# Decoder block on 8 cores: tables of the second half built early and kept in DRAM, halo projections in another order

## The chip, the cores and the metric

The program runs on the 8 cores of one Trainium2 chip, the same program on each with other data and no traffic between cores. Each core computes 2048 tokens of one sequence (4 sequences, two cores for each). The metric is the device time in microseconds (us) of the slowest core.

## The reference

One decoder layer over tokens of width 1024. What is computed:

```
h = x + 0.5*SwiGLU_1(rmsnorm(x))            # width 2816
u = rmsnorm(h);  z = u @ W_in               # [conv GLU | q | k | v | merge gates]
A = conv module (GLU, causal depthwise conv 31 wide, LayerNorm, swish, C->D)
q, k = rotary(q, cos, sin), rotary(k, cos, sin)     # cos, sin of positions*inv_freq
B = 12 heads of 128, 3 groups with dilation 1, 4, 16;
    query t attends to t - j*dilation, j = 0..128;  groups merged by softmax denominators
h = h + W_o(sigmoid(gA)*yA + sigmoid(gB)*yB)
h = h + 0.5*SwiGLU_2(rmsnorm(h))
h = h + sigmoid(rmsnorm(h) @ W_pg) * (p @ W_pp);  y = rmsnorm(h)
```

The tokens just ahead of a core's own 2048 (128, 512 or 2048 of them by group) are needed as keys and values too. They are called the halo here. A core computes them itself from `xh`, the 2048 tokens before its own.

## The kernel before

All activations lie transposed, channels on 128 partitions and tokens along the free axis; `H` is the float32 residual, `U` its normed bf16 copy, each 8 tiles of 128 channels by 2048 tokens, worked on in blocks of 512 tokens. The kernel goes through stages in this order:

- **Halo part.** Load `xh`, FFN 1, RMSNorm into `U` (line 480). Then two rotary tables for the halo's tokens are built: `build_tables` (line 387) loads 1 MB of positions with an SP DMA, does twenty-one 128x2048 passes on DVE, of which the last is a multiply by a sign, and two Sin activations on ACT, into `cos2` and `sinS` (`t_71`, `t_72`; the positions are `t_74`). Lines 494 to 519 then run over 12 heads, and for each do a K projection with rotary (`proj_rot`, line 403: for each block of up to 512 tokens 8 matmuls, an ACT copy, a permuting matmul, three DVE operations), a store of the result to `khd` in DRAM, a V projection (`proj_v`, line 421: for each 128 tokens 8 matmuls of 128 columns and a copy out of PSUM that alternates between DVE and ACT), and a store to `vhd`. Heads 0 to 3 have a halo of 128 tokens, 4 to 7 of 512, 8 to 11 of 2048. Lines 521 to 533 compute the conv branch's 32 halo columns. A barrier follows.
- **Own part.** Load `xo`, FFN 1, RMSNorm, a barrier (546), `build_tables` for the core's own tokens (557), another barrier (558). Then the projections of head 0 (`proj_rot_g`, `proj_v_g`), and the attention of a head woven with the projections of the next. After this the conv, the merge, FFN 2, the last gates and the output.

Order is written out by hand: `Sched` (line 33) keeps one list per engine in program order, and each engine works its list in that order. An operation waits by semaphores for the earlier writers and readers of its tiles. A DMA is issued by its engine's list too, so one that waits holds up those behind it: plain loads and all stores are on SP's list, and weight loads, which cast float32 to bf16, are on POOL's (`pool_load`). A barrier makes the next operation of each engine wait for the last of all engines and for all DMAs so far. Weights come in chunks of 128 output columns (`load_w_chunk`, line 464) into a ring of 4 tiles in the halo part and of 3 in the own part: a chunk's load waits until the matmuls of the chunk in its tile are done. PSUM has 8 banks of one tile each, taken in turn.

Of the kernel before, what the change touches and what calls it, by code (L numbers as in the profile page):

```python
# [8 lines left out]
F32 = mybir.dt.float32  # L9
BF16 = mybir.dt.bfloat16  # L10
I32 = mybir.dt.int32
# [4 lines left out]
NT = 2048  # L16
# [8 lines left out]
GROUPS = ((1, 16), (4, 4), (16, 1))  # L25
# [166 lines left out]
def _build_body(nc, dbg):  # L192
    S = None
# [18 lines left out]
    yT = nc.dram_tensor("yT", [D, NT], F32, kind="ExternalOutput").ap()  # L212
    khd = nc.dram_tensor("khd", [12, 128, NT], BF16, kind="Internal").ap()
    vhd = nc.dram_tensor("vhd", [12, 128, 16, 128], BF16, kind="Internal").ap()
    dbg_out = None
    if dbg:
        dbg_out = nc.dram_tensor("dbg", [D, NT], F32, kind="ExternalOutput").ap()

    S = Sched(nc)
    A = Arena(nc, 229376)  # L220
# [3 lines left out]
    def set_pool(banks):  # L224
        ps_pool["banks"] = list(banks)
        ps_pool["i"] = 0

    def ps_next():
        bk = ps_pool["banks"]
        i = bk[ps_pool["i"] % len(bk)]  # L230
        ps_pool["i"] += 1
        return PS[i], ("ps", i)
# [17 lines left out]
    def sp_load(dst, src, key, grp):  # L250
        S.op("sp", lambda e: e.dma_start(out=dst, in_=src), writes=[key], dma=grp)

    def pool_load(dst, src, key, grp):
        S.op("pool", lambda e: e.dma_start(out=dst, in_=src), writes=[key], dma=grp)  # L254
# [20 lines left out]
    def checkpoint(name):  # L275
        if STOP == name:
            yv_ = yT.rearrange("(c p) t -> p c t", p=128)
            for c in range(8):
                S.op("sp", lambda e, c=c: e.dma_start(out=yv_[:, c, :], in_=H[:, c, :]),
                     reads=[("H", c, b) for b in range(NB)], dma="yout")  # L280
            S.finish()
            S.emit()
            raise _Stop()

    def mm(out, lhsT, rhs, start, stop, reads, writes):
        S.op("pe", lambda e: e.matmul(out, lhsT=lhsT, rhs=rhs, start=start, stop=stop), reads, writes)  # L286

    def act(out, in_, func, reads, writes, bias=None, scale=None):
        kw = {}
        if bias is not None:  # L290
            kw["bias"] = bias
        if scale is not None:
            kw["scale"] = scale
        S.op("act", lambda e: e.activation(out=out, in_=in_, func=func, **kw), reads, writes)  # L294

    def tt(eng, out, in0, in1, op, reads, writes):
        S.op(eng, lambda e: e.tensor_tensor(out=out, in0=in0, in1=in1, op=op), reads, writes)  # L297

    def stt(eng, out, in0, scalar, in1, op0, op1, reads, writes):
        S.op(eng, lambda e: e.scalar_tensor_tensor(out=out, in0=in0, scalar=scalar, in1=in1, op0=op0, op1=op1), reads, writes)  # L300

    def ts(eng, out, in0, s1, s2, op0, op1, reads, writes):
        if s2 is None:
            S.op(eng, lambda e: e.tensor_scalar(out=out, in0=in0, scalar1=s1, scalar2=None, op0=op0), reads, writes)  # L304
        else:
            S.op(eng, lambda e: e.tensor_scalar(out=out, in0=in0, scalar1=s1, scalar2=s2, op0=op0, op1=op1), reads, writes)  # L306

    def cp(eng, out, in_, reads, writes):
        if eng == "act":
            S.op(eng, lambda e: e.copy(out=out, in_=in_), reads, writes)  # L310
        else:
            S.op(eng, lambda e: e.tensor_copy(out=out, in_=in_), reads, writes)  # L312
# [74 lines left out]
    def build_tables(cos2, sinS, pcol0, tmp_f, tmp_i, tmp_k):  # L387
        sp_load(tmp_i[:], pos[:, pcol0:pcol0 + NT], "tmp_i", "tab")
        for tab, key, shift in ((sinS, "sinS", 0.0), (cos2, "cos2", math.pi / 2)):
            cp("dve", tab[:], tmp_i[:], ["tmp_i"], [key])  # L390
            ts("dve", tab[:], tab[:], invf, shift, ALU.mult, ALU.add, [key, "sm"], [key])
            ts("dve", tmp_f[:], tab[:], 1.0 / TWO_PI, None, ALU.mult, None, [key], ["tmp_f"])
            cp("dve", tmp_k[:], tmp_f[:], ["tmp_f"], ["tmp_k"])
            cp("dve", tmp_f[:], tmp_k[:], ["tmp_k"], ["tmp_f"])
            stt("dve", tab[:], tmp_f[:], -TWO_PI, tab[:], ALU.mult, ALU.add, ["tmp_f", key], [key])
            ts("dve", tmp_f[:], tab[:], math.pi, -TWO_PI, ALU.is_gt, ALU.mult, [key], ["tmp_f"])
            tt("dve", tab[:], tab[:], tmp_f[:], ALU.add, [key, "tmp_f"], [key])
            ts("dve", tmp_f[:], tab[:], -math.pi, TWO_PI, ALU.is_lt, ALU.mult, [key], ["tmp_f"])
            tt("dve", tab[:], tab[:], tmp_f[:], ALU.add, [key, "tmp_f"], [key])
            act(tab[:], tab[:], AF.Sin, [key], [key])  # L400
        ts("dve", sinS[:], sinS[:], sgn, None, ALU.mult, None, ["sinS", "sm"], ["sinS"])
# [16 lines left out]
            tt("dve", t2[:, 0:n], pw[:, 0:n], sinS[:, tsl], ALU.mult, [pwk, "sinS"], [t2k])  # L418
            tt("dve", dst[:, o0:o0 + n], t1[:, 0:n], t2[:, 0:n], ALU.add, [t1k, t2k], [(dst_key, o0 // BL)])

    def proj_v(wt, wk, dst, dst_key, tile_starts, d, vring_keys=None):
        for i, st0 in enumerate(tile_starts):
            pv, pvk = ps_next()
            bs = sorted({(st0 + d * q) // BL for q in (0, 127)})
            bs = list(range(bs[0], bs[-1] + 1))
            for c in range(8):
                mm(pv[:, 0:128], U[:, c, st0:st0 + 127 * d + 1:d], wt[:, c, :],
                   c == 0, c == 7, [wk] + [("U", c, b) for b in bs], [pvk])
            cp("act" if i % 2 else "dve", dst[:, i, :], pv[:, 0:128], [pvk], [(dst_key, i)])

    def proj_rot_g(wt, wk, dst, dst_key, t0, ntok, cos2, sinS, qb_ring, t_ring):
        for o0 in range(0, ntok, BL):
# [31 lines left out]
    def load_w_chunk(ring, col0, ncol=128):  # L464
        wt, wk = ring.next()
        wt = wt[:, 0:8 * ncol].rearrange("p (c n) -> p c n", c=8)
        pool_load(wt, w_in_v[:, :, col0:col0 + ncol], wk, "%s%d" % wk)
        return wt, wk

    QOFF, KOFF, VOFF, GOFF = 2048, 2048 + 1536, 2048 + 3072, 2048 + 4608  # L470
# [11 lines left out]
    cos2 = A.alloc([128, NT], F32)  # L482
    sinS = A.alloc([128, NT], F32)
    tmp_f = A.alloc([128, NT], F32)
    tmp_i = A.alloc([128, NT], I32)
    tmp_k = A.alloc([128, NT], I32)
    build_tables(cos2, sinS, 0, tmp_f, tmp_i, tmp_k)
    checkpoint("p0b")
    wring = Ring(A, "w", int(os.environ.get("KW", "4")), [128, 8 * 128], BF16)
    qb_ring = Ring(A, "qb", 2, [128, BL], BF16)  # L490
    t_ring = Ring(A, "t", 4, [128, BL], F32)
    kst_ring = Ring(A, "kst", 2, [128, NT], BF16)
    vst_ring = Ring(A, "vst", 2, [128, 16, 128], BF16)
    for g, (d, nbl) in enumerate(GROUPS):
        nh = 128 * d
        for j in range(4):
            head = 4 * g + j
            if head < int(os.environ.get("KSKIP", "0")):
                continue
            wt, wk = load_w_chunk(wring, KOFF + head * 128)  # L500
            kst, kstk = kst_ring.next()
            proj_rot(wt, wk, kst, kstk, NT - nh, nh, cos2, sinS, qb_ring, t_ring)
            if not os.environ.get("KNOSTORE"):
              S.op("sp", lambda e, kst=kst, head=head, nh=nh: e.dma_start(out=khd[head, :, 0:nh], in_=kst[:, 0:nh]),
                 reads=[(kstk, i) for i in range((nh + BL - 1) // BL)], writes=[("khd", head)], dma="hstk%d" % kstk[1])
            if head == 0:
                checkpoint("p0c")
            wt, wk = load_w_chunk(wring, VOFF + head * 128)
            vst, vstk = vst_ring.next()
            starts = [NT - nh + r for r in range(d)]  # L510
            proj_v(wt, wk, vst, vstk, starts, d)
            if not os.environ.get("KNOSTORE"):
              S.op("sp", lambda e, vst=vst, head=head, d=d: e.dma_start(out=vhd[head, :, 0:d, :], in_=vst[:, 0:d, :]),
                 reads=[(vstk, i) for i in range(d)], writes=[("vhd", head)], dma="hstv%d" % vstk[1])
            if head == 0:
                checkpoint("p0d")
            if head == 11:
                checkpoint("p0e")
            checkpoint("p0h%d" % head)
    sg_ring = Ring(A, "sg", 2, [128, BL], F32)  # L520
    for c in range(8):
        wa, wak = load_w_chunk(wring, c * 128)
# [27 lines left out]

    cos2 = A.alloc([128, NT], F32)
    sinS = A.alloc([128, NT], F32)
    mark3 = A.off
    tmp_f = A.alloc([128, NT], F32)
    tmp_i = A.alloc([128, NT], I32)
    tmp_k = A.alloc([128, NT], I32)
    build_tables(cos2, sinS, NT, tmp_f, tmp_i, tmp_k)
    S.barrier()
    A.off = mark3
    set_pool([0, 1, 2, 3])  # L560
    wring = Ring(A, "w", 3, [128, 8 * 128], BF16)
    qb_ring = Ring(A, "qb", 2, [128, BL], BF16)
# [125 lines left out]
    wring = Ring(A, "w", 3, [128, 8 * 128], BF16)  # L688
# [64 lines left out]
    wring = Ring(A, "w", 2, [128, 8 * 128], BF16)  # L753
# [70 lines left out]
    for b in range(NB):  # L824
# [21 lines left out]
        for c in range(8):  # L846
# [3 lines left out]
                 reads=[("H", c, b)], dma="yout")  # L850
# [89 lines left out]
```

How the kernel before makes its waits and increments, by code:

```python
                def body(eng):  # L122
                    waited = {}
                    for o in self.ops[e]:
                        ws = {}
                        for d in o.deps:
                            if not self._needs(o, d):
                                continue
                            if d.is_dma:
                                key, sem, val = "d_" + d.grp, self.groups[d.grp][0], d.val
                            else:
                                key, sem, val = "s_" + d.eng, sems[d.eng], d.count
                            if waited.get(key, 0) >= val:
                                continue
                            if key not in ws or ws[key][1] < val:
                                ws[key] = (sem, val)
                        for key, (sem, val) in ws.items():
                            eng.wait_ge(sem, val)
                            waited[key] = val
                        inst = o.fn(eng)
                        if o.is_dma:
                            inst.then_inc(self.groups[o.grp][0], 16)
                        elif o.need_inc:
                            inst.then_inc(sems[e], 1)
```

## Time and profile before

| | us |
|---|---|
| median of 2 runs | 3450.42 (3449.57 to 3451.27) |
| profiled execution | 3456.62 |
| its span on the slowest core (core 4) | 3455.1 |
| spans of the 8 cores | 3432.3 to 3455.1 |

| engine | busy us | share of the span |
|---|---|---|
| PE matmul | 2759.9 | 80% |
| DVE | 1382.4 | 40% |
| ACT | 818.9 | 24% |
| POOL | 190.4 | 6% |

The shares are averages over stages that have different limits. What counts below are the stretches in which PE stands still, and what ends them. Times inside the execution are given in us from the start of core 4's span.

### The profile page before, as it was taken

To read this page: it belongs to the slowest core of one execution; us is meant where nothing else is said; L and a number is where in the kernel's file an instruction comes from. 1 tells how busy PE (TensorE), PEld (TensorE's weight loads), DVE (VectorE), ACT (ScalarE), POOL (GpSimd) and SP (SyncE) were. 2 spreads that over 40 slices of the span, in tenths; PEclk is the share of its full clock that TensorE was granted. 3 is DMA by queue.
4 is the path that set the end of the run, shared out by engine and by line. 5 is a ranking of instruction groups with operands and counts; after the bars stand their busy time and mean duration, and the time that the engine had idled before them with its cause. 6 is when DMAs were issued, how large, how long until landed. Compare 5 with 4: busy or idle time off the path is not lost.

```text
span 3455.1 us, 41479 instructions; the slowest of 8 cores (3432.3 to 3455.1 us)
## 1 busy us (share of the span) xinstructions
PE 2759.9 (80%) x14139; PEld 1305.8 (38%) x14360; DVE 1382.4 (40%) x2050; ACT 818.9 (24%) x1744; POOL 190.4 (6%) x228
## 2 busy tenths in 40 slices
PE   4999993655999991787777677747749989999977
PEld 1444440441444440454454433313324434444422
DVE  4131338424232337567667710130043353313267
ACT  3101012113101003222222244344421121010144
POOL 0000000120000000000000000000001010000010
PEclk9999995876999995999898888979979989999988
DMA  8131202877122100221121021112124252222042
GB/s 175 25 49 25 31 1 28 87 99 156 26 48 37 19 1 13 31 32 20 29 32 20 16 28 17 15 12 19 10 24 41 28 72 45 37 38 31 1 43 98
DMA packets 222233, 134.67 MB, mean 39 GB/s; under 512 B 165584, under 2 KB 204880, under 8 KB 219728
## 3 DMA queue, kind: packets, MB, share of 16 engines
q0 software_dynamic: 207488, 93.57, 23.6%
q1 hardware_dynamic: 14544, 38.44, 3.4%
q8 instruction: 124, 2.03, 0.2%
q14 instruction: 77, 0.63, 0.1%
HBM read 211.65 MB, written 13.89 MB: 65 GB/s over the span
## 4 chain that ended last, share of the span: by engine, by line
PE 69%; DVE 12%; ACT 9%; DMA 5%; issue 4%; SPq 0%; ACTq 0%; DVEq 0%; POOL 0%; POOLq 0%
PE ps L286 69%; ACT t L294 8%; DVE t L300 4%; DVE t L297 3%; DVE t L329 2%; DMA t<-w_in 2%; DVE t L660 2%; DMA t<-xh 1%; DMA t<-xo 1%; DVE t L312 1%; DMA t<-vhd 1%; DVE t L306 0%; ACT t L310 0%; DMA t<-w_co 0%; SPq L317 0%
## 5 line engine op out<-in xcount | busy, mean ns | idle before, releaser
L286 PE MATMUL ps<-t,t 128*128 128x512 bf16 (+1 forms) x14139 | 2759.9, 352 | 679.6 <-ACT t L294 319.4
L286 PEld LDWEIGHTS ps<-t,t 128*128 128x128 bf16 x14360 | 1305.8, 105 | 2133.1 <-issue 986.9
L297 DVE TENSOR_TENSOR t<-t,ps 128x512 bf16<-128x512 f32 (+3 forms) x688 | 388.4, 569 | 1175.6 <-PE ps L286 897.3
L294 ACT ACTIVATE t<-ps 128x512 f32<-128x512 f32 (+2 forms) x712 | 379.3, 534 | 1761.2 <-PE ps L286 1690.6
L300 DVE SCALAR_TENSOR_TENSOR t<-ps,t 128x512 f32<-128x512 f32 x292 | 202.0, 692 | 257.7 <-PE ps L286 254.9
L294 ACT ACTIVATE t<-t 128x512 bf16<-128x512 f32 (+1 forms) x260 | 159.7, 644 | 394.4 <-DVE t L300 130.9
L297 DVE TENSOR_TENSOR t<-ps,t 128x512 f32<-128x512 f32 (+1 forms) x240 | 154.1, 675 | 155.2 <-ACT t L294 153.7
L254 POOL DMA_DIRECT2D t<-w_in x124 | 108.9, 880 | 1784.0 <-PE ps L286 1264.7
L297 DVE TENSOR_TENSOR t<-t,t 128x512 bf16<-128x512 f32 (+5 forms) x228 | 191.2, 844 | 22.4 <-DVE t L297 0.7
L294 ACT ACTIVATE t<-t,t 128x128 bf16<-128x128 bf16 (+1 forms) x516 | 169.1, 415 | 26.3 <-DVE t L297 14.7
L300 DVE SCALAR_TENSOR_TENSOR t<-t,t,t 128x512 bf16<-128x512 f32 (+1 forms) x224 | 150.9, 746 | 3.0
L329 DVE RECIPROCAL t<-t 128x512 f32<-128x512 f32 x24 | 80.3, 3348 | 123.3 <-ACT t L294 123.3
L304 DVE TENSOR_SCALAR t<-ps,t 128x512 f32<-128x512 f32 x32 | 24.0, 752 | 232.1 <-PE ps L286 224.9
L310 ACT CAST t<-t 128x32 bf16<-128x32 f32 (+1 forms) x64 | 26.5, 414 | 188.8 <-DVE t L304 145.4
L294 ACT ACT_TABLE_LOAD x28 | 35.9, 1283 | 124.4 <-DVE t L297 79.3
L310 ACT CAST t<-ps 128x128 bf16<-128x128 f32 x136 | 36.2, 266 | 111.4 <-PE ps L286 111.4
L312 DVE CAST t<-ps 128x128 bf16<-128x128 f32 x140 | 38.6, 287 | 40.9 <-PE ps L286 40.8
L660 DVE RECIPROCAL t<-t 128x2048 f32<-128x2048 f32 x4 | 51.8, 12953 | 0.4
L312 DVE COPY t<-ps 128x128 f32<-128x128 f32 x128 | 36.4, 290 | 19.1 <-PE ps L286 10.5
L254 POOL DMA_DIRECT2D t<-w1g x12 | 10.6, 886 | 552.4 <-PE ps L286 541.1
L294 ACT ACTIVATE t<-ps,t 128x512 f32<-128x512 f32 x28 | 19.2, 687 | 16.1 <-PE ps L286 16.0
L845 DVE RECIPROCAL t<-t 128x512 f32<-128x512 f32 x4 | 13.4, 3353 | 21.7 <-ACT t L294 21.7
(26 smaller groups left out, 137.9 us busy)
## 6 DMA issues: line engine op xcount, KB each, us to landing
t<-w_in POOLq DMA_DIRECT2D x124, 256.0 KB, 5.5
t<-w1g POOLq DMA_DIRECT2D x10, 1024.0 KB, 10.9
t<-w1u POOLq DMA_DIRECT2D x10, 1024.0 KB, 16.2
t<-w1d POOLq DMA_DIRECT2D x10, 1024.0 KB, 14.4
t<-xh SPq DMA_DIRECT2D x8, 1024.0 KB, 19.5
t<-xo SPq DMA_DIRECT2D x8, 1024.0 KB, 20.4
yT<-t SPq DMA_DIRECT2D x32, 256.0 KB, 3.2
t<-w2g POOLq DMA_DIRECT2D x5, 1024.0 KB, 11.8
```

What stands on the lines that cost most here:

```text
L254: S.op("pool", lambda e: e.dma_start(out=dst, in_=src), writes=[key], dma=grp)
L286: S.op("pe", lambda e: e.matmul(out, lhsT=lhsT, rhs=rhs, start=start, stop=stop), reads, writes)
L294: S.op("act", lambda e: e.activation(out=out, in_=in_, func=func, **kw), reads, writes)
L297: S.op(eng, lambda e: e.tensor_tensor(out=out, in0=in0, in1=in1, op=op), reads, writes)
L300: S.op(eng, lambda e: e.scalar_tensor_tensor(out=out, in0=in0, scalar=scalar, in1=in1, op0=op0, op1=op1), reads, writes)
L304: S.op(eng, lambda e: e.tensor_scalar(out=out, in0=in0, scalar1=s1, scalar2=None, op0=op0), reads, writes)
L310: S.op(eng, lambda e: e.copy(out=out, in_=in_), reads, writes)
L312: S.op(eng, lambda e: e.tensor_copy(out=out, in_=in_), reads, writes)
L329: S.op("dve", lambda e, rt=rt: e.reciprocal(out=rt[:], in_=rt[:]), [rtk], [rtk])
L660: S.op("dve", lambda e: e.reciprocal(out=DEN[:], in_=DEN[:]), ["DEN"], ["DEN"])
L845: S.op("dve", lambda e, rt=rt: e.reciprocal(out=rt[:], in_=rt[:]), [rtk], [rtk])
```

## The change

- A DRAM tensor `tabd` for two 1 MB tables is added.
- In the halo part the loop over heads is split into two: first all 12 V projections with their stores, then all 12 K projections with theirs. The V tiles are all copied out of PSUM by ACT (`act_only`).
- Between the two loops `build_tables` is run for the own tokens, the tables are stored to `tabd`, and then it is run for the halo's tokens in the same tiles.
- In the own part `build_tables` and the barrier behind it are gone, and two loads from `tabd` stand in their place.

```diff
+    tabd = nc.dram_tensor("tabd", [2, 128, NT], F32, kind="Internal").ap()
...
-            cp("act" if i % 2 else "dve", dst[:, i, :], pv[:, 0:128], [pvk], [(dst_key, i)])
+            cp("act" if (i % 2 or act_only) else "dve", dst[:, i, :], pv[:, 0:128], [pvk], [(dst_key, i)])
...
-    build_tables(cos2, sinS, 0, tmp_f, tmp_i, tmp_k)
-    checkpoint("p0b")
-    wring = Ring(A, "w", int(os.environ.get("KW", "4")), [128, 8 * 128], BF16)
+    wring = Ring(A, "w", 4, [128, 8 * 128], BF16)
...
+            wt, wk = load_w_chunk(wring, VOFF + head * 128)
+            vst, vstk = vst_ring.next()
+            starts = [NT - nh + r for r in range(d)]
+            proj_v(wt, wk, vst, vstk, starts, d, act_only=True)
+            S.op("sp", lambda e, vst=vst, head=head, d=d: e.dma_start(out=vhd[head, :, 0:d, :], in_=vst[:, 0:d, :]),
+                 reads=[(vstk, i) for i in range(d)], writes=[("vhd", head)], dma="hstv%d" % vstk[1])
+    build_tables(cos2, sinS, NT, tmp_f, tmp_i, tmp_k)
+    S.op("sp", lambda e, t_=cos2: e.dma_start(out=tabd[0], in_=t_[:]), reads=["cos2"], writes=["tabd0"], dma="tst0")
+    S.op("sp", lambda e, t_=sinS: e.dma_start(out=tabd[1], in_=t_[:]), reads=["sinS"], writes=["tabd1"], dma="tst1")
+    build_tables(cos2, sinS, 0, tmp_f, tmp_i, tmp_k)
+    for g, (d, nbl) in enumerate(GROUPS):
+        nh = 128 * d
+        for j in range(4):
+            head = 4 * g + j
             wt, wk = load_w_chunk(wring, KOFF + head * 128)
             kst, kstk = kst_ring.next()
             proj_rot(wt, wk, kst, kstk, NT - nh, nh, cos2, sinS, qb_ring, t_ring)
...
-            wt, wk = load_w_chunk(wring, VOFF + head * 128)
-            vst, vstk = vst_ring.next()
-            starts = [NT - nh + r for r in range(d)]
-            proj_v(wt, wk, vst, vstk, starts, d)
...
-    mark3 = A.off
-    tmp_f = A.alloc([128, NT], F32)
-    tmp_i = A.alloc([128, NT], I32)
-    tmp_k = A.alloc([128, NT], I32)
-    build_tables(cos2, sinS, NT, tmp_f, tmp_i, tmp_k)
-    S.barrier()
-    A.off = mark3
+    sp_load(cos2[:], tabd[0], "cos2", "tld0")
+    sp_load(sinS[:], tabd[1], "sinS", "tld1")
```

SP's list in the halo part, before. `t_74` is the tile of positions, `t_86` and `t_87` are the staging tiles of K, `t_88` and `t_89` those of V.

```order
L317 DMA t_52<-xh 128x2048 x8
L251 DMA t_74<-pos 128x2048
L504 DMA khd<-t_86 128x128
L513 DMA vhd<-t_88 128x128
L504 DMA khd<-t_87 128x128
```

The same list from the last V stores on, with the change (`t_71` is `cos2`, `t_72` is `sinS`).

```order
L501 DMA vhd<-t_88 128x2048
L501 DMA vhd<-t_89 128x2048
L501 DMA vhd<-t_88 128x2048
L501 DMA vhd<-t_89 128x2048
L252 DMA t_74<-pos 128x2048
L504 DMA tabd<-t_71 128x2048
L505 DMA tabd<-t_72 128x2048
L252 DMA t_74<-pos 128x2048
L514 DMA khd<-t_86 128x128
```

The load of positions stood ahead of all stores of the part. It now stands behind the twelve V stores, and the second one behind the two table stores.

ACT's list with the change, from the copies of the last V heads on. The four rows on 128x2048 are the Sin activations of the two builds, and those that write `t_80` and `t_81` are the copies of the K projections.

```order
L311 CAST t_88<-ps 128x128 x16
L311 CAST t_89<-ps 128x128 x16
L295 ACTIVATE t_72<-t_72 128x2048
L295 ACTIVATE t_71<-t_71 128x2048
L295 ACTIVATE t_72<-t_72 128x2048
L295 ACTIVATE t_71<-t_71 128x2048
L295 ACTIVATE t_80<-ps 128x128
```

All V copies moved ahead of the Sin activations, and both builds' Sin activations stand ahead of the first K copy.

## Rows read from the trace of the kernel before

**Rows 1.** Chain that ended last (page, part 4): shares by engine

```profile
PE 69%; DVE 12%; ACT 9%; DMA 5%; issue 4%; SPq 0%; ACTq 0%; DVEq 0%; POOL 0%; POOLq 0%
```

**Rows 2.** Timeline, halo build: start us, us, engine, line, operation, count, [idle before <-releaser]

```profile
527.53 0.33 SPq L251 DMA_DIRECT2D t<-pos  x1
529.07 3.56 POOL L254 DMA_DIRECT2D t<-w_in  x4 [126.30 <-ACT t L294]
...
567.23 0.27 PE L286 MATMUL ps<-t,t 128*128 128x128 bf16 x1 [10.60 <-DVE t L300]
...
571.53 1.22 DVE L312 CAST t<-t 128x2048 f32<-128x2048 int32 x1
571.76 0.26 PE L286 MATMUL ps<-t,t 128*128 128x128 bf16 x1 [0.40 <-DVE t L300]
572.57 0.88 POOL L254 DMA_DIRECT2D t<-w_in  x1 [39.94 <-PE ps L286]
...
604.83 1.91 ACT L294 ACTIVATE t<-t 128x2048 f32<-128x2048 f32 x1 [13.20 <-DVE t L297]
...
607.05 1.99 PE L286 MATMUL ps<-t,t 128*128 128x128 bf16 x17 [35.03 <-ACT t L294]
```

**Rows 3.** Timeline, build of the own part

```profile
1332.65 5.39 DVE L300 SCALAR_TENSOR_TENSOR t<-t,t,t 128x512 bf16<-128x512 f32 x8
1338.77 0.33 SPq L251 DMA_DIRECT2D t<-pos  x1
1343.84 1.23 DVE L312 CAST t<-t 128x2048 f32<-128x2048 int32 x1 [5.79 <-DMA t<-pos]
...
1377.07 1.91 ACT L294 ACTIVATE t<-t 128x2048 f32<-128x2048 f32 x1 [13.42 <-DVE t L297]
...
1380.37 2.67 POOL L254 DMA_DIRECT2D t<-w_in  x3 [210.34 <-issue]
1385.05 3.57 PE L286 MATMUL ps<-t,t 128*128 128x512 bf16 x8 [61.84 <-DMA t<-w_in]
...
1389.56 3.93 PE L286 MATMUL ps<-t,t 128*128 128x512 bf16 x9 [0.95 <-ACT t L294]
```

**Rows 4.** Timeline, weight chunks of the conv halo, four issued together

```profile
735.38 3.50 POOL L254 DMA_DIRECT2D t<-w_in  x4 [8.72 <-PE ps L286]
743.21 1.01 PE L286 MATMUL ps<-t,t 128*128 128x128 bf16 x8 [7.42 <-DMA t<-w_in]
...
749.07 1.01 PE L286 MATMUL ps<-t,t 128*128 128x128 bf16 x8 [1.37 <-DMA t<-w_in]
```

**Rows 5.** Chain in order of time, last V projection: start us, us, what

```profile
726.08 8.39 PE ps L286 x129
```

**Rows 6.** Timeline, PE: ninth matmul of a 128-token K, blocks of 512 tokens

```profile
612.12 0.27 PE L286 MATMUL ps<-t,t 128*128 128x128 bf16 x1 [0.57 <-ACT t L294]
...
697.30 2.10 PE L286 MATMUL ps<-t,t 128*128 128x512 bf16 x9 [0.89 <-ACT t L294]
700.24 2.10 PE L286 MATMUL ps<-t,t 128*128 128x512 bf16 x9 [0.84 <-ACT t L294]
```

**Rows 7.** Stretches: engines' busy us (count), granted clock, DMA share, GB/s

```profile
572.00:606.00 34.00, 0.02 (x1) 0.00 (x0) 31.68 (x21) 4.36 (x3) 0.88 (x1) 0.50 0.08 8
620.00:640.00 20.00, 15.19 (x106) 9.42 (x109) 6.18 (x13) 2.86 (x7) 5.26 (x6) 0.70 1.04 99
657.00:667.00 10.00, 6.98 (x35) 3.17 (x36) 6.75 (x11) 1.79 (x3) 0.88 (x1) 1.00 0.01 1
607.05:734.70 127.65, 95.78 (x882) 65.95 (x889) 54.95 (x116) 23.31 (x63) 19.27 (x22) 0.88 0.69 86
1342.00:1343.00 1.00, 0.00 (x0) 0.00 (x0) 0.00 (x0) 0.00 (x0) 0.00 (x0) 0.50 0.95 401
```

**Rows 8.** Stores of the last four heads, 512 KB each, landing: vhd, then khd

```profile
DMA to landing us min/median/max: 2.7/2.7/3.5
DMA to landing us min/median/max: 4.0/4.3/4.9
```

**Rows 9.** Tile xh, eight loads of 1 MB: landing

```profile
DMA to landing us min/median/max: 5.3/19.5/32.5
```

**Rows 10.** Groups by form, 607 to 735 us

```profile
L310 ACT CAST t<-ps 128x128 bf16<-128x128 f32 x40 | 10.6, 266 | 41.8 <-PE ps L286 41.8
```

More of the change, by code:

```diff
@@ L419, in proj_rot, with proj_v @@
             tt("dve", dst[:, o0:o0 + n], t1[:, 0:n], t2[:, 0:n], ALU.add, [t1k, t2k], [(dst_key, o0 // BL)])
-    def proj_v(wt, wk, dst, dst_key, tile_starts, d, vring_keys=None):
+    def proj_v(wt, wk, dst, dst_key, tile_starts, d, vring_keys=None, act_only=False):
         for i, st0 in enumerate(tile_starts):
@@ L497, in _build_body @@
             head = 4 * g + j
-            if head < int(os.environ.get("KSKIP", "0")):
-                continue
+            wt, wk = load_w_chunk(wring, VOFF + head * 128)
[12 more added lines that the diff above has]
+            head = 4 * g + j
             wt, wk = load_w_chunk(wring, KOFF + head * 128)
@@ L502, in _build_body @@
             proj_rot(wt, wk, kst, kstk, NT - nh, nh, cos2, sinS, qb_ring, t_ring)
-            if not os.environ.get("KNOSTORE"):
-              S.op("sp", lambda e, kst=kst, head=head, nh=nh: e.dma_start(out=khd[head, :, 0:nh], in_=kst[:, 0:nh]),
+            S.op("sp", lambda e, kst=kst, head=head, nh=nh: e.dma_start(out=khd[head, :, 0:nh], in_=kst[:, 0:nh]),
                  reads=[(kstk, i) for i in range((nh + BL - 1) // BL)], writes=[("khd", head)], dma="hstk%d" % kstk[1])
-            if head == 0:
-                checkpoint("p0c")
-            wt, wk = load_w_chunk(wring, VOFF + head * 128)
-            vst, vstk = vst_ring.next()
-            starts = [NT - nh + r for r in range(d)]
-            proj_v(wt, wk, vst, vstk, starts, d)
[L512 to L519, printed above, removed]
     sg_ring = Ring(A, "sg", 2, [128, BL], F32)
```

## The prediction

> **What bounds the kernel now.** I read the chain of waits first. It lies 69% on PE, 12% on DVE and 9% on ACT [rows 1]: PE sets the end, and a DVE stage counts where PE stands behind it. The change touches two such places, so I read the timeline around both.
>
> At the halo build PE's last matmul before the stall, one of head 0's K, starts at 571.76, DVE builds from 571.53, the second Sin starts at 604.83 and takes 1.91, and PE resumes at 607.05 after 35.03 us idle [rows 2]. The load of positions went out at 527.53 and was long in by then, so this build costs **35.2 us** (571.53 to 606.74), and nothing covers it.
>
> At the own part's build the load goes out at 1338.77, DVE starts at 1343.84 (5.1 us, the load's latency), the last Sin ends at 1378.98, the weights are issued only behind the barrier at 1380.37, and PE starts at 1385.05 after 61.84 us idle [rows 3]. So 46.3 us lie between the load's issue and the first matmul.
>
> Between them, K and V of the halo take 607.05 to 734.7, 127.65 us at a mean clock of 0.88 [rows 7].
>
> **The change, step by step**, on the time axis of the trace of before.
>
> *V projections first.* V of heads 0 to 3 needs nothing but `U` and the four chunks issued at 529.07 [rows 2]. PE starts at 567.23, follows `U`'s last block to 572.0, and does the other three heads in 1.01 us each (the length of 8 matmuls at the low clock [rows 4]): 575. The fifth chunk goes out at 572.57 as it does today [rows 2]; four issued together reached PE 7.8 us after the issue and then every 2 us (743.21 to 749.07) [rows 4]. So V4 starts near 580.4 and V7's weights are in by 586.5. A V4-type head is 32 matmuls: 4 us at the low clock (1.01 for 8), 2.1 at the high (8.39 for 129 [rows 5]). With the clock rising on the way, V7 ends near 593, and the chunk of V8, sent when V4 is done, is in by then. V8 to V11 take 4 x 8.4 = 33.6 us: PE done at **627**, and 622 or 640 if the clock rises at once or only in the middle of V9. ACT alone copies a tile in 0.27 us [rows 10], while PE makes one in 0.52 (8.39 x 8/129), so `act_only` costs nothing; if ACT fell behind, 8 banks would give 4 us of slack. The store of V8 must land before V10 is copied, and 512 KB lands in 2.7 us [rows 8]: no stall.
>
> *The build is not beside the V stage.* SP works in order, and the load of positions stands behind the last V store, which waits for the last copy. It is issued at 627.8 and lands 5.1 us later [rows 3], 6 with that store ahead of it: DVE starts at **633.8** (bounds 632.9 and 637). Then 35.2 us: Sin done at **669.0**. DVE is idle all through the V stage; this is what the order of SP's list takes away.
>
> *Stores and second load.* SP issues the cosine's store, the sine's store and the second load of positions together at 669. The three megabytes go through the same 16 engines. One load takes 5.1 us [rows 3], of which most is transfer, at up to 401 GB/s [rows 7], 2.6 us for 1 MB. I take 5.1 + 2 x 2.8 + 1.0 for the three issues = about **12 us**. Bounds: 5.1 if reads and writes do not hinder each other, and 22 if each store costs twice the 4.3 us that 512 KB of `khd` needed [rows 8] (2 x 8.6 + 5.1). The xh loads, eight in 32.5 us [rows 9], 4.1 each, would make it 14, which is why I stay near 12. The Trainium skill (DMA: Bandwidth & Descriptors, "Anatomy of one DMA") speaks against spilling, since completion of a write to HBM can be surprisingly slow, and gives 2.0 us plus bytes at 436 GB/s; by that the gap is an estimated 9.2 us and the total 3 us lower. No run here shows a 1 MB store.
>
> *Halo build.* Starts at 681.0, again 35.2: **716.2**, PE resumes at 716.5 instead of 607.05.
>
> *K projections alone.* K0's matmuls are done during the wait. K1 to K3: 1.01 for the eight matmuls [rows 4], 0.57 for ACT's copy and 0.27 for the ninth [rows 6], 1.85 each, 5.6 us. K4 to K7: 4.7 us for the first (3.57 for 8 matmuls at the low clock [rows 3], then 0.95 for ACT's copy [rows 3] and some 0.2 to 0.4 for the ninth), 3 to 4 for the others as the clock rises and chunks arrive: 14.8 us. K8 to K11: 16 blocks of 2.95 us (697.30 to 700.24 [rows 6]), 47.2. With the first piece 0.8, **68.4** (65 to 75). Four such blocks in a row ran at clock 1.00 with PE 70% busy [rows 7], so K without V between does not fall to 1.2 GHz. The stage ends at 784.9 where it ended at 734.7: **+50.2**. The conv halo finds three of its chunks loaded, as today. Checked from the other side: one more build 35.2, first load 6, gap 12, less 3 by which V and K are shorter apart than woven.
>
> *Own part.* DVE's build, its load and the second barrier go. The norm ends at 1338.04 (1332.65 + 5.39 [rows 3]), and weight chunks follow the barrier there with POOL's delay of 1.4 (1378.98 to 1380.37 [rows 3]), at 1339.4, and reach PE 4.7 us later [rows 3]: 1344.1, were they alone. Two tables of 1 MB move at the same time, up to 5.6 us of transfer; I add half, 2.6: PE at **1346.7**, **-38.3** (bounds -41 alone and -33 behind both tables and POOL late). The Trainium skill (same page, "Issuing engines are not separate DMA queues") says that SP's and POOL's transfers run on the same 16 engines; without it the first bound would stand. The sine table is in by 1350, and the first product with it is due at 1352. The loads of `khd` and `vhd` behind the tables have the whole of head 0's projections as cover. Without that cover they would add their 2 us.
>
> **Sum.** +50.2 - 38.3 = **+11.9 us**. Against the profiled 3456.6 that is 3468.5; the two runs shown have a median 6.2 below the profiled execution, so I predict **3462 us**. In words: one build moves from one exposed place to another. Added are the round trip through DRAM and the load of positions in the halo part; saved is that load in the own part.
>
> **The rivals.**
> - *V covers the first build.* If the load of positions were out early (it was at 527.53 before [rows 2]), DVE would build from 571.5 while PE does V, and only the Sins would wait for ACT's V copies until 627. 633 + 12 + 35.2 = 680 instead of 716: 36 us less, **3426**. Against it: SP's list as printed. Chance 0.04.
> - *The clock stays low in the split loops* (slower). The wait of some 90 us leaves PE at 0.50, as in 572 to 606 [rows 7], and after it come short heads with weight waits, in which the clock was only 0.70 on average [rows 7]. If PE stayed at 1.2 GHz through V8 to V11 and K8 to K11: 512 matmuls of 128 columns by 0.126 - 0.065 (1.01/8 [rows 4] less 8.39/129 [rows 5]) = 31 us, and 16 K blocks of 9 matmuls by 3.57/8 - 2.10/9 = 0.21 each = 30 us. Together +61, **3523**, 2.1% over before. It decides if the clock is not at 1.00 by V8. Against: the four K blocks at 1.00 [rows 7] and V's dense stream. Chance 0.03.
> - *DRAM traffic is slow.* Eight cores store 2 MB and load 1 MB at one moment. At the bound of 22 us, with V at 640 and the own part at -33: 11.9 + 10 + 13 + 5 = +40, **3490**. Chance 0.10.
> - *A gain in the gap*: stores and load beside each other (5 us), V at 622, own part -41: 11.9 - 7 - 5 - 3 = -3, **3447**. Chance 0.08, part of the same mechanism as the forecast.
> - The forecast, 3450 to 3478: 0.75.
>
> **Numbers.** 2% is 69 us, about what a measurement of this kernel tells from no change: 3381 or 3519. Only the clock rival passes the upper limit, just, and nothing here passes the lower one. Faster 0.01, same 0.97, slower 0.02. The range is 3443 to 3485, which leaves out the first two rivals and half of the slow one.
>
> **What the new profile would show.** A PE idle stretch of some 88 us between V and K, with DVE busy twice for 35 us and idle for 12 between. Positions issued just behind the last `vhd` store. First V copy on ACT near 568, last near 627. PE resuming near 716 and leaving the K loop near 785. In the own part from the end of the norm to the first matmul 8 to 9 us instead of 47. I am wrong if DVE is busy with a table before V11 is done, if the gap between the builds is over 20 us, or if the clock in V8 to V11 or K8 to K11 is under 0.9.

## The result

The change made the kernel 0.36% slower: the ratio to before is 1.0036, with a 95% interval of 1.002 to 1.0051, about 12 us of 3450. That is no change by the 2% bound, and close to the +11.9 us forecast (as a time, 3462 us). The medians over all runs are 3471.39 and 3450.42 us; single runs in which cores of a die ran at a lower clock lie in these medians, so the ratio, which leaves them out, is the number to go by. The profiled execution took 3466.64 us, 10.0 more than that of before, and its slowest core is again core 4.

### The profile page after: what moved, and what is told of

Read it like the earlier page. It is cut to its first block, busy times and chain, and to the rows that moved or that the text cites. A ratio compares the mean times of both kernels' runs of the same rounds, so it can differ in the third digit from the quotient of the medians.

```text
span 3465.1 us, 41548 instructions; the slowest of 8 cores (3445.3 to 3465.1 us)
## 1 busy us (share of the span) xinstructions
PE 2744.2 (79%) x14141; PEld 1302.0 (38%) x14360; DVE 1370.6 (40%) x2006; ACT 827.4 (24%) x1787; POOL 190.4 (5%) x228
## 4 chain that ended last, share of the span: by engine, by line
PE 68%; DVE 12%; ACT 9%; DMA 5%; issue 4%; SPq 0%; ACTq 0%; DVEq 0%; POOL 0%; POOLq 0%
PE ps L287 68%; ACT t L295 8%; DVE t L301 4%; DVE t L298 3%; DVE t L330 2%; DVE t L651 1%; DMA t<-w_in 1%; DMA t<-xh 1%; DMA t<-xo 1%; DVE t L313 1%; DMA vhd<-t 1%; DMA t<-pos 1%; DVE t L307 0%; ACT t L311 0%; DMA t<-vhd 0%
## 5 line engine op out<-in xcount | busy, mean ns | idle before, releaser
L287 PE MATMUL ps<-t,t 128*128 128x512 bf16 (+2 forms) x14141 | 2744.2, 351 | 706.0 <-ACT t L295 373.2
L330 DVE RECIPROCAL t<-t 128x512 f32<-128x512 f32 x24 | 80.3, 3347 | 123.9 <-ACT t L295 123.9
L311 ACT CAST t<-ps 128x128 bf16<-128x128 f32 x180 | 46.3, 268 | 120.7 <-PE ps L287 99.7
L651 DVE RECIPROCAL t<-t 128x2048 f32<-128x2048 f32 x4 | 51.8, 12953 | 0.4
L313 DVE CAST t<-t 128x2048 f32<-128x2048 int32 (+1 forms) x12 | 14.7, 1226 | 80.4 <-DMA t<-pos 79.6
L313 DVE COPY t<-ps 128x128 f32<-128x128 f32 x128 | 36.4, 290 | 19.7 <-PE ps L287 10.9
L255 POOL DMA_DIRECT2D t<-w1g x12 | 10.6, 886 | 555.6 <-PE ps L287 541.2
L313 DVE CAST t<-ps 128x128 bf16<-128x128 f32 x96 | 26.4, 285 | 16.6 <-PE ps L287 16.6
L295 ACT ACTIVATE t<-ps,t 128x512 f32<-128x512 f32 x28 | 19.2, 687 | 16.2 <-PE ps L287 15.2
## 6 DMA issues: line engine op xcount, KB each, us to landing
t<-w1g POOLq DMA_DIRECT2D x10, 1024.0 KB, 12.6
```

The lines of the kernel that those rows point to most:

```text
L330: S.op("dve", lambda e, rt=rt: e.reciprocal(out=rt[:], in_=rt[:]), [rtk], [rtk])
L651: S.op("dve", lambda e: e.reciprocal(out=DEN[:], in_=DEN[:]), ["DEN"], ["DEN"])
```

## The profile after

Span and clock of core 4, then the timeline of the halo part on SP, DVE, ACT and PE (rows picked out; they answer to [rows 2]):

```profile
core 4: 3465.1 us, clock 0.907
```

```profile
574.35 57.73 SPq L501 DMA_DIRECT2D vhd<-t  x12
...
632.13 0.75 SPq L252 DMA_DIRECT2D t<-pos  x1
640.52 1.23 DVE L313 CAST t<-t 128x2048 f32<-128x2048 int32 x1 [67.47 <-DMA t<-pos]
...
673.83 1.91 ACT L295 ACTIVATE t<-t 128x2048 f32<-128x2048 f32 x1 [13.20 <-DVE t L298]
675.81 0.32 SPq L504 DMA_DIRECT2D tabd<-t  x1
676.22 0.39 SPq L505 DMA_DIRECT2D tabd<-t  x1
676.70 0.86 SPq L252 DMA_DIRECT2D t<-pos  x1
687.03 1.23 DVE L313 CAST t<-t 128x2048 f32<-128x2048 int32 x1 [12.10 <-DMA t<-pos]
...
719.98 1.91 ACT L295 ACTIVATE t<-t 128x2048 f32<-128x2048 f32 x1 [14.47 <-DVE t L298]
```

DVE stands idle for 67.47 us, through the whole V stage, and what ends the wait is the load of positions that SP issued only behind the twelfth V store. Then come build, 11.3 us of gap, build. PE's view of it, as stretches with the same columns as [rows 7], from the V stage to the conv halo:

```profile
599.00:632.00 33.00, 32.65 (x488) 32.50 (x488) 0.00 (x0) 16.99 (x67) 2.63 (x3) 0.92 0.46 80
632.00:722.00 90.00, 0.00 (x0) 0.00 (x0) 64.32 (x42) 9.04 (x6) 1.76 (x2) 0.52 0.23 58
731.00:742.00 11.00, 7.50 (x32) 2.93 (x33) 7.03 (x11) 2.39 (x4) 3.50 (x4) 1.00 1.01 116
742.00:788.00 46.00, 32.24 (x138) 13.10 (x138) 30.62 (x47) 8.96 (x15) 2.62 (x3) 1.00 0.37 64
```

PE does nothing for 90 us where it did nothing for 35, and DVE is busy in 64 of them. The K loop without V between ran at clock 1.00 once it was past its short heads.

The own part, timeline (answers to [rows 3]):

```profile
1386.34 5.39 DVE L301 SCALAR_TENSOR_TENSOR t<-t,t,t 128x512 bf16<-128x512 f32 x8
1392.01 0.80 SPq L252 DMA_DIRECT2D t<-tabd  x2
1392.76 2.67 POOL L255 DMA_DIRECT2D t<-w_in  x3 [169.28 <-issue]
...
1404.24 3.57 PE L287 MATMUL ps<-t,t 128*128 128x512 bf16 x8 [27.22 <-DMA t<-w_in]
```

From the norm's end (1391.73) to the first matmul 12.5 us instead of 47.0. The weight chunk, not a table, is what PE waits for, and it needs 11.5 us from its issue where it needed 4.7 before. As means of the eight cores that is 9.9 us against 4.8.

The stages read from the timelines of all eight cores, as means in us. "Halo" is from the end of the halo's norm to the first load of `xo`, "V" from that end to PE's long stall, "own" from SP's first issue behind the own norm to the first projection matmul, "rest" from that matmul to the last load of `vhd`.

| kernel | halo | V | stall | own | rest |
|---|---|---|---|---|---|
| before | 190.1 | | 35.0 | 46.5 | 563.9 |
| before, again (e8) | 190.8 | | 35.0 | 46.7 | 563.5 |
| the change | 247.8 | 54.1 | 89.4 | 10.6 | 558.5 |
| the change, again (e10) | 242.6 | 51.8 | 88.2 | 10.6 | 562.2 |
| e1 positions early | 204.8 | 50.7 | 51.9 | 10.6 | 561.1 |
| e2 six V tiles | 239.6 | 49.7 | 87.9 | 10.1 | 560.6 |
| e3 split only | 200.5 | 54.3 | 43.5 | 45.6 | 561.4 |
| e4 own part alone | 194.0 | | 35.1 | 10.9 | 561.7 |
| e5 no gap | 231.8 | 51.5 | 77.0 | 10.6 | 560.2 |
| e9 copies alternate | 244.3 | 52.0 | 88.1 | 10.6 | 560.5 |

Two profiles of one kernel differ by up to 5 us in the halo stage and 4 in the rest, so smaller differences between rows say nothing. Halo less stall is what V, K and the conv halo take: 155.1 and 155.8 us woven (before), 152.9 to 158.4 in the six split versions with two staging tiles for V, 155.6 as their mean.

## The experiments

**e1, positions early.** SP loads the own positions ahead of the V loop.

```diff
+    sp_load(tmp_i[:], pos[:, NT:2 * NT], "tmp_i", "tab")
     wring = Ring(A, "w", 4, [128, 8 * 128], BF16)
...
-    build_tables(cos2, sinS, NT, tmp_f, tmp_i, tmp_k)
+    build_tables(cos2, sinS, NT, tmp_f, tmp_i, tmp_k, load=False)
```

> The changed kernel with one edit: the load of the own positions is issued by SP ahead of the V loop instead of behind it. Theory (the order of SP's list keeps the first build from lying beside the V projections): DVE builds from about 573 us beside PE's V work and is through its passes near 607; only the two Sins wait on ACT for the V copies, until about 632; the sign multiply, stores and second load follow. PE's idle time between V and K falls from 91 us to 52 to 56, and the kernel is 35 to 38 us shorter than the changed one: about 3426, ratio to before 0.993. Rival (it is ACT's list, with the Sins behind the V copies, or the DMA traffic that holds the build): idle time 80 us or more, kernel 3455 or more.

The one run compared took 3420.36 us, and those of before on that chip lay between 3444 and 3458. In its timeline (core 1, the slowest), a DVE pass of the build lies beside the V matmuls, and the Sins come behind the last V copy:

```profile
571.04 1.22 DVE L313 CAST t<-t 128x2048 f32<-128x2048 int32 x1
...
594.72 31.62 PE L287 MATMUL ps<-t,t 128*128 128x128 bf16 x488 [2.43 <-ACT t L311]
...
602.67 2.29 DVE L298 TENSOR_TENSOR t<-t,t 128x2048 f32<-128x2048 f32 x1
626.27 1.28 ACT L295 ACT_TABLE_LOAD   x1
627.56 3.71 ACT L295 ACTIVATE t<-t 128x2048 f32<-128x2048 f32 x2
...
632.23 0.99 SPq L252 DMA_DIRECT2D t<-pos  x1
642.95 1.23 DVE L313 CAST t<-t 128x2048 f32<-128x2048 int32 x1 [12.09 <-DMA t<-pos]
...
678.11 1.14 PE L287 MATMUL ps<-t,t 128*128 128x128 bf16 x9 [51.77 <-ACT t L295]
```

The stall is 51.9 instead of 89.4 us. One line that moves one DMA in SP's list is worth 36 to 37.5 us of PE's time (88.2 and 89.4 less 51.9): the theory holds. The order of ACT's list costs only the two Sins and their table load.

**e2, six staging tiles for V.**

```diff
-    vst_ring = Ring(A, "vst", 2, [128, 16, 128], BF16)
+    vst_ring = Ring(A, "vst", 6, [128, 16, 128], BF16)
```

> The changed kernel with 6 staging tiles for V instead of 2, so that no V copy waits for the store of two heads before. Theory (the small stores of heads 0 to 7, 8 us from issue to landing beside the weight loads, hold ACT and then PE through the ring of 2): ACT's waits for vhd stores vanish (8 to 21 us by core in the changed kernel), V8 starts 4 to 8 us earlier on the late cores, and the kernel is 4 to 6 us shorter than the changed one: about 3457. Rival (weight chunks bound V4 to V7 anyway): V8 starts within 2 us of the changed kernel's 599, kernel 3462 to 3464.

What is tested here is a wait that the changed kernel has and before has not. Who waited for whom in its V stage (us in total, times, longest), core 4:

```profile
ACT t L311 <- DMA vhd<-t: 20.9, 6, 5.7
PE ps L287 <- ACT t L311: 7.1, 3, 4.2
```

and the timeline rows of it:

```profile
592.73 2.18 PE L287 MATMUL ps<-t,t 128*128 128x128 bf16 x32 [1.22 <-ACT t L311]
598.66 0.77 ACT L311 CAST t<-ps 128x128 bf16<-128x128 f32 x4 [5.68 <-DMA vhd<-t]
599.07 32.65 PE L287 MATMUL ps<-t,t 128*128 128x128 bf16 x488 [4.16 <-ACT t L311]
```

With six tiles no such wait is left on any of the eight cores, and V takes 49.7 us as a mean instead of 54.1 and 51.8: 2 to 4 us. The ratio to before, 1.0034 (1.0017 to 1.0051), cannot be told from the change's 1.0036. The wait is real and the stage puts its price at 2 to 4 us. The 4 to 6 us that the theory gave the kernel's time are not seen there.

**e3, the split alone.** V loop, then the halo's build, then the K loop; the own build where it was.

```diff
-    build_tables(cos2, sinS, NT, tmp_f, tmp_i, tmp_k)
-    S.op("sp", lambda e, t_=cos2: e.dma_start(out=tabd[0], in_=t_[:]), reads=["cos2"], writes=["tabd0"], dma="tst0")
-    S.op("sp", lambda e, t_=sinS: e.dma_start(out=tabd[1], in_=t_[:]), reads=["sinS"], writes=["tabd1"], dma="tst1")
     build_tables(cos2, sinS, 0, tmp_f, tmp_i, tmp_k)
...
```

> V loop and K loop apart, as in the change, but only the halo's tables are built between them; the own tables are built in the own part as before, and nothing goes to DRAM. Theory (the halo part's extra 58 us are 35 for one more build, 11 for the stores and the second load, and 12 for the split itself: the exposed load of positions, 8, and V and K no shorter apart than woven): halo part 11 to 13 us longer than before, own part unchanged, kernel 3461 to 3463, ratio 1.0033. Rival (V and K apart are shorter than woven, as the prediction had it with 3 us less, so the split costs 5 us): kernel 3455, ratio 1.0013.

The load of positions goes out behind the last V store, and DVE and PE wait for it (core 4):

```profile
624.88 1.18 SPq L251 DMA_DIRECT2D t<-pos  x1
631.92 1.23 DVE L312 CAST t<-t 128x2048 f32<-128x2048 int32 x1 [61.76 <-DMA t<-pos]
...
667.46 1.14 PE L286 MATMUL ps<-t,t 128*128 128x128 bf16 x9 [42.92 <-ACT t L294]
```

The halo stage is 200.5 us, 10.0 over the mean of the two profiles of before and just under the theory's 11 to 13. The stall is 43.5: the build's 35.1 plus 8.4 for the load of positions, now exposed. So only 1.6 us are left for V and K apart against woven, less than two profiles of one kernel differ by; nothing says that one way is longer than the other. The two runs compared, 3450.82 and 3452.36, are 4 to 6 us over the median of before's on that chip (3446.6), where the theory had 11 to 13 and the rival 5. The stage speaks against the 3 us gain that the prediction gave the split, and so does the mean of six split versions under the table above, 155.6 us against 155.1 and 155.8; the kernel's time speaks for the rival, and two runs do not settle it.

**e4, the own part alone.** The kernel before, with the stores placed behind its one halo build, and the own part of the change. The own tables are not built at all: what the own part loads are the halo's, so the output is wrong and only the time counts.

> The kernel before, with the own part of the change alone: the tables are loaded from DRAM instead of built. What is stored there are the halo's tables, right after their build in the halo part, so the own tokens are rotated by the halo's angles; it is a measurement of time only. Theory (the own part's gain is 36 us, PE starting 10 to 12 us after the norm instead of 47): halo part unchanged within 2 us since the stores lie beside the projections, kernel 36 us shorter than before: 3414, ratio 0.9896. If the attention stage's further 5 us in the changed kernel come with the change too: 3409. Rival (the tables' loads are in part given back by the late weight chunk and by the late sine table): less than 32 us.

Ratio 0.9897 (0.9865 to 0.9929), 35.5 us faster. "Own" is 10.9 us against 46.6: -35.7. The rows on core 4, from the norm's end at 1320.65:

```profile
1321.37 0.80 SPq L252 DMA_DIRECT2D t<-tabd  x2
1322.10 2.67 POOL L255 DMA_DIRECT2D t<-w_in  x3 [170.19 <-issue]
...
1330.99 3.18 PE L287 MATMUL ps<-t,t 128*128 128x512 bf16 x8 [25.61 <-DMA t<-w_in]
```

The part of the change that removes the own build is worth 36 us, and both its loads' costs are in that. The halo stage came out 3.5 us longer (194.0 against 190.4), where the theory allowed 2; one profile does not tell that from scatter.

**e5, no gap.** The own tables get tiles of their own, and the halo's positions are loaded ahead of the V loop.

```diff
+    cosN = A.alloc([128, NT], F32)
+    sinN = A.alloc([128, NT], F32)
+    tmp_iN = A.alloc([128, NT], I32)
+    sp_load(tmp_i[:], pos[:, 0:NT], "tmp_i", "tab")
...
-    build_tables(cos2, sinS, NT, tmp_f, tmp_i, tmp_k)
+    build_tables(cosN, sinN, NT, tmp_f, tmp_iN, tmp_k, kp="N", kc="cosN", ks="sinN")
...
+    build_tables(cos2, sinS, 0, tmp_f, tmp_i, tmp_k, load=False)
...
```

The stores take `cosN` and `sinN`, and a small ring of the conv halo is made narrower for room.

> The changed kernel, but the own tables are built in tiles of their own, and the halo's positions are loaded into their own tile before the V loop, so the halo build waits neither for the two table stores nor for a load. Theory (the 11.3 us between the builds are the three megabytes in flight, and nothing else is held by the stores): the two builds follow each other without idle time on DVE, PE's stall falls from 89 us to 77 to 79, kernel 11 us shorter than the changed one: about 3450, the same as before. Rival (a store to DRAM beside it slows the rest, or the second build is held by ACT's Sins): stall 84 us or more.

Stall 77.0 us, 11 to 12 less; ratio 0.9993 (0.9975 to 1.0011). Its DVE goes from one build to the next at once, while the stores are issued (core 0):

```profile
666.72 1.91 ACT L295 ACTIVATE t<-t 128x2048 f32<-128x2048 f32 x1 [13.19 <-DVE t L298]
667.74 1.22 DVE L313 CAST t<-t 128x2048 f32<-128x2048 int32 x1
668.71 0.32 SPq L509 DMA_DIRECT2D tabd<-t  x1
```

So the whole loss of the change is the size of that gap: without it the kernel equals before. PE's stall shows no time for the stores once nothing waits for their tiles. The run takes away two waits at once, for the stored tiles and for the second load. In the change's rows on core 4 the sine's store landed at 685.0 (8.8 us after its issue) and the load at 686.9, so the stores by themselves would have held DVE for some 9 of the 11 us, if they had landed no sooner without the load.

**e9, V copies on both engines.**

```diff
-            proj_v(wt, wk, vst, vstk, starts, d, act_only=True)
+            proj_v(wt, wk, vst, vstk, starts, d)
```

> The changed kernel with the V copies alternating between DVE and ACT as before. Theory (ACT at 0.27 us a tile was never the limit of a tile every 0.52, so act_only is worth nothing): V stage 49 to 58 us by core as in the changed kernel, mean within 2 us of 54.1, kernel within 0.1% of the changed one. Rival (ACT alone, held by stores of the small heads, passes that wait on to PE, which two engines would not): V stage mean 51 or less, kernel 3 us shorter.

V 52.0 us, inside the change's two values (54.1 and 51.8); the runs compared took 3465.23 and 3471.63, the change itself 3470.09 there (e10), before 3446 to 3456. No cost of `act_only` shows, and the waits for the stores fall on DVE as well as on ACT.

**e8 and e10, both kernels once more.**

> The kernel before once more, for its profile. Theory (the 9 us by which the changed kernel's attention and later stages were shorter are scatter between profiled executions): from the first matmul of the own part to the last vhd load 560 to 564 us as a mean of the cores, and from there to the first output 1417 to 1420, where the changed kernel had 558.5 and 1417.5. Rival (the change makes attention faster): 564 or more again.

> The changed kernel once more, for its profile. Theory (its stages as means of eight cores are steady): from the end of the halo's norm to the load of xo 246 to 249 us, of which V 53 to 55 and the stall 89 to 90; own part's first matmul 10 to 12 us behind the load of the tables; from there to the last vhd load 558 to 561 us, 3 to 5 shorter than the 564 and 563 of the two profiles of the kernel before. Rival (the shorter attention stage was scatter of one execution): 563 or more.

Before gave 3454.88 us, the change 3470.09. The theory of e8 came out (563.5 and 1418.4 us). That of e10 did so for the own part only: the halo stage came out 3.4 us under its range, V 1.2 and the stall 0.8, so these stages are less steady from profile to profile than it took them to be. From the first pair of profiles to the second, the shortening of all that comes behind the own part's first matmul fell from 8.8 us (rest 563.9 to 558.5, and from there to the first output 1420.9 to 1417.5) to 3.7 (563.5 to 562.2, and 1418.4 to 1416.0). So more than half of it was scatter. For the stage behind the first matmul the theory's 558 to 561 was missed by 1 us, and the rival's 563 was not reached. Before's two values still lie above all eight others of the table, even above e3's, whose own part is that of before. On the other hand e6 below, which loads its own tables as the change does, has 563.3, all but the same as before. Whether a few us of it belong to the change is not settled.

**e6, both builds woven into the FFNs.** This is where the experiments point: e1 shows that DVE's build costs nothing beside busy PE, and the FFN has the most room.

```diff
+    def tables_gen(tset, pcol0):
...
                         tt("dve", ACTB[:, jj, blk(b)], st[:], pu[:], ALU.mult, [stk, puk], [("A", jj, b)])
+                        next(gen, None)
...
+    sp_load(cos2[:], tabd[0], "cos2", "tld0")
+    sp_load(sinS[:], tabd[1], "sinS", "tld1")
+    rmsnorm_to_U(G_MIX, sq_ring, rt_ring)
...
-    build_tables(cos2, sinS, NT, tmp_f, tmp_i, tmp_k)
...
```

`tables_gen` does for each 512 tokens a load, 20 DVE passes, two Sins, the sign and two stores; `next(gen, None)` lets it go on by one pass. The barrier behind the own build is gone too.

> The kernel before, with both sets of tables built in pieces of 512 tokens inside the FFNs ahead of their use, one DVE pass after each SwiGLU product, the pieces stored to DRAM and loaded as whole tables at the start of the next stage, beside its RMSNorm. K and V stay woven. Theory (PE bounds the FFN, DVE and ACT have room there, so both builds cost nothing): halo part 35 us shorter, own part 40 us shorter (first matmul 7 us after the norm instead of 47), FFNs within 3 us of before, kernel 3372, ratio 0.978. Rival (DVE's passes and ACT's table switches between Silu and Sin hold up the copies out of PSUM in the FFN): FFNs 10 us or more longer each and the kernel above 3390.

Ratio 0.9768 (0.9719 to 0.9816), 80 us faster. The first halo FFN as one stretch, first in this kernel (core 1), then in before (core 4):

```profile
80.00:527.00 447.00, 445.26 (x2060) 201.49 (x2060) 163.69 (x272) 55.56 (x94) 10.42 (x12) 1.00 0.23 32
```

```profile
80.00:527.00 447.00, 442.83 (x2019) 201.46 (x2059) 128.38 (x187) 51.35 (x86) 9.97 (x12) 1.00 0.18 25
```

DVE does 35.3 us more in the same 447 us, ACT 4.2 more, and PE's clock and pace are unchanged; the halo's norm starts 0.5 us later as a mean of the cores (537.3 against 536.8). The second FFN is 1 to 2 us longer. The halo stage falls to 160.8 us, 30 less, where the theory had 35: without the stall the projections and the conv halo take some 5 us more than with it, and no run shows why. From the own norm's end to the first matmul it is 6.5 us instead of 47.3, as forecast.

**e7, and no barrier behind the own norm.**

```diff
     rmsnorm_to_U(G_MIX, sq_ring, rt_ring)
-    S.barrier()
-    A.off = mark3
```

> The same as e6_woven, and the barrier behind the own part's RMSNorm is gone, since its tiles are no longer reused; the first weight chunks load during the norm. Theory (the wait left there is the barrier and the chunk's latency, 7 us): first matmul of the own part during the norm, kernel 7 to 12 us shorter than e6_woven: about 3362. Rival (DVE's list has the norm's passes ahead of the first rotation, so an early PE only waits elsewhere): 3 us or less.

Ratio 0.9757 (0.9719 to 0.9795). This is the fastest version, 84 us below before by the ratio and faster than the change too. Against e6 the intervals overlap; the runs compared are 3360.24, 3362.70, 3364.16 and 3376.92, those of e6 3365.13, 3374.12 and 3385.39. PE starts during the norm, then waits for DVE (core 1):

```profile
1292.90 0.38 PE L287 MATMUL ps<-t,t 128*128 128x512 bf16 x1 [0.84 <-ACT t L295]
1295.41 5.39 DVE L301 SCALAR_TENSOR_TENSOR t<-t,t,t 128x512 bf16<-128x512 f32 x8
1300.72 1.28 DVE L298 TENSOR_TENSOR t<-ps,t 128x512 f32<-128x512 f32 x2
1301.55 3.57 PE L287 MATMUL ps<-t,t 128*128 128x512 bf16 x8 [8.27 <-DVE t L298]
```

The rival's mechanism, DVE's norm passes ahead of the first rotation, is there (8.27 us), so part of the gain is lost. The times of the kernels do not resolve the rest. The two profiles do: from the end of the own norm to the first output there are 1987.9 us in e6 and 1972.4 here, as means of eight cores, while two profiles of one kernel differ by under 3 there (2032.0 and 2029.3 before, 1986.9 and 1989.5 with the change).

## Why the prediction was right

The forecast, +11.9 us, and the measured ratio, about +12 us, agree. Its terms beside those of the trace on core 4:

| term | forecast | measured, core 4 |
|---|---|---|
| V stage, norm's end to PE done | 55.4 | 58.7 (573.06 to 631.72) |
| load of own positions to DVE | 6.0 | 8.4 (632.13 to 640.52) |
| own build | 35.2 | 35.2 (to 675.74) |
| gap between the builds | 12 | 11.3 (to 687.03) |
| halo build | 35.2 | 34.9 (to 721.89) |
| K stage | 68.4 | 67.2 (722.20 to 789.4) |
| halo part, whole | +50.2 | +53.5 |
| own part | -38.3 | -34.5 |

- *The build is not beside V.* Right, and shown by e1: the rival "V covers the first build" was ruled out by SP's list and by nothing else. The 36 us worked out for it came out as 36 to 37.5.
- *Stores and second load.* Right in size. The gap was 12 by the neighbouring rows and 11.3 measured. The second load landed 10.2 us after its issue. The estimate from the Trainium skill (DMA: Bandwidth & Descriptors, "Anatomy of one DMA"), 9.2 us for the three megabytes, was 2.1 short of the gap; its fit is given for single DMAs that GpSimd issues, and these three were SP's. e5 shows that this gap is as large as the change's whole loss.
- *V stage.* The step that failed is "512 KB lands in 2.7 us: no stall". It priced the stores of the long heads and passed over those of the short ones, which are issued while weight chunks are in flight and hold the ring of two. V took 3.3 us more than forecast on core 4, and e2 puts the wait at 2 to 4. The trace of before had it: there, from 608 to 655 us on core 4, these stores landed after 6.3 to 7.6 us and not 2.7 (size, median us to landing):

```profile
vhd<-t SPq DMA_DIRECT2D x4, 128.0 KB, 7.6
vhd<-t SPq DMA_DIRECT2D x4, 32.0 KB, 6.3
```

- *Clock.* Right: 0.92 through V8 to V11, 1.00 in the K loop from 731 us on. The slow rival did not come about.
- *K stage and split.* The K stage was sized well. The cross-check gave the split 3 us: 6 for the load less 3 by which V and K are shorter apart than woven. e3 puts it at 10, 8.4 of them the load, and the 3 us are not seen with two staging tiles. With six (e2) V, K and the conv halo take 151.7 us, 3 to 4 less than woven, in one profile.
- *Own part.* The mechanism was right, the term mis-sized: -38.3 forecast, -35.7 as a mean of the cores (e4). I gave the chunk 2.6 us for the tables beside it ("half" of 5.6 would be 2.8); on core 4 it took 6.8 more. As means of the eight cores it took 4.6 to 4.8 us in before and e3, 9.9 and 10.2 in the change and e4, where the tables load beside it, and 5.5 in e6, where they do not. So the tables cost the chunk about 5 us. From the norm's end to the first matmul the forecast had 8 to 9 us, and the cores' mean is 11.
- *The sum.* At the own part's first matmul core 4 is 19.2 us late instead of 11.9: the halo part was forecast 3.3 too short and the own part's gain 3.8 too large. That the end result still fitted is owed to the stages behind it, which I had at zero, and so in part to luck. With two profiles of each kernel, as means of eight cores: halo +54.8, own -36.0, rest -3.3, last stages -2.9, together +12.6, which is the measured ratio. The forecast's total was right partly because a halo part 4.6 us too short and an own gain 2.3 too large stood against 6.2 us behind them that nothing in the change explains.

## What to carry to other kernels

Work that is to lie beside another stage must be followed through every in-order list that it touches, the DMA issue list too: here one load, waiting in SP's list behind stores that did not concern it, turned an overlap of 35 us into none. Moving a stall of PE to another place gains nothing; it has to be moved under work of another engine, and the stage to choose is the one that PE bounds with the most idle time on the engine in question, in pieces small enough to slip between its copies. When a tile is stored to DRAM and at once written again, the transfer is exposed, here 9 us for two stores of 1 MB, and the load behind them made it 11; a second set of tiles and an early load removed both.

## What the runs showed of the hardware that was not expected

Small stores beside several weight loads landed later than large ones beside one. DMA issues of the change, 560 to 640 us on core 4: size, median us to landing:

```profile
vhd<-t SPq DMA_DIRECT2D x4, 512.0 KB, 3.2
t<-pos SPq DMA_DIRECT2D x1, 1024.0 KB, 8.3
vhd<-t SPq DMA_DIRECT2D x4, 128.0 KB, 6.8
vhd<-t SPq DMA_DIRECT2D x4, 32.0 KB, 6.8
```

A 32 KB store took 6.8 us beside the weight chunks of the short heads and a 512 KB store 3.2 in the time of the long ones, where one or two chunks move. It goes with the traffic and not with the size. Over all eight cores the V stores of 32, 128 and 512 KB that were issued with at most one weight chunk in flight landed after 2.8, 2.5 and 3.4 us (medians), those of 32 and 128 KB issued with more chunks in flight after 7.4 and 5.9; all of 512 KB are of the first kind. So a landing time is read from a neighbour with the same traffic around it, not from the same size. The same goes for loads: 1 MB of positions took 8.3 us with a V store and two weight chunks in flight, 5.1 alone [rows 3].
